# Attention inside a projection loop: own PSUM space for scores, rotary partners 64 rows apart, v stored twice

## The chip, the cores and the metric

One core of a Trainium2 chip runs the whole program. The metric is the time of one execution on the device in microseconds (us). TensorE (PE) multiplies, VectorE (DVE) and ScalarE (ACT) do the elementwise work, GpSimd (POOL) clears buffers, and SyncE (SP) issues the loads of weights. Each engine has its own stream of instructions, and they meet at semaphores.

## What is computed

Two layers over 256 tokens of width 2048, in fp32. Layer 0 mixes tokens by attention with 32 query heads and 4 key heads of width 64, rotary positions, a sink per head and a window of two chunks of 64; layer 1 by a recurrent block. Each is followed by a squared-ReLU MLP of width 8192. The change touches the attention alone:

```python
def rope(x, pos):
    half = x.shape[-1] // 2
    ...
    x1, x2 = xf[..., :half], xf[..., half:]
    out = jnp.concatenate([x1 * cos - x2 * sin, x2 * cos + x1 * sin], axis=-1)

    qkv = h @ w_qkv + b_qkv
    ...
    q = rope(q, pos)
    k = rope(k, pos)
    ...
    scores = jnp.where(valid, scores, NEG_INF)
    ...
    probs = jax.nn.softmax(jnp.concatenate([scores, sink], axis=-1), axis=-1)[..., :-1]
    out = jnp.einsum('bckgqs,bcskd->bcqkgd', probs.astype(v.dtype), v_band)
    out = out.reshape(B, S, N_HEADS * HEAD_DIM)
    return out @ w_o + b_o
```

## The kernel before

**Weights.** All projections stream 512 KB chunks of fp32 weights. ScalarE rounds a chunk to the fp32r type (`split_hi`, L343), VectorE takes the rest (`split_lo`, L766), and TensorE multiplies both parts. A *pair* is 256 output columns over all 16 row tiles: four `products` calls (s = 0 to 3) of 16 matmuls each, here called chunks of the pair. `next_hi` and `next_lo` prepare chunk s for the following pair as soon as the present pair has used its chunk s, since `w_hi` and `w_lo` hold one pair. At a pair's end ScalarE copies one half of the sum out of PSUM (`copy_half`, L356) and VectorE adds the other (`add_halves`, L780).

**The stage.** The projection to q, k and v is five quads of two pairs, q = 0 to 4. Quad 0 gives k and v. Of the others, each pair gives 256 columns of queries, which is four heads. Attention for the j-th such group runs one pair later, woven into the next pair's chunks. j = 0 lies in the pair (1, 1), j = 1 to 6 in the six pairs of quads 2 to 4, and j = 7 in the first quad of the output projection (`late_quad`, which has an order of its own). One *step* is one pair with the attention of one j.

**A step on TensorE.** Behind chunk 1: `rotate(j + 1)`, an fp32 product with a permutation matrix `swap` that puts each head's rotary partner, 32 rows away, in place, and `transpose_probs(j - 1)`, 8 transposes. Behind chunk 2: `scores(j)`, 24 matmuls of 256 columns, and `attend(j - 1)`, 24 matmuls of 128 columns. There, of two heads one takes rows 0 to 63 of the output and one rows 64 to 127. So `vcur` holds v between two blocks of zeros, and a slice of it that starts at v or in front of it sends v to the one half of the rows or the other. Scores and transposed probabilities share the two PSUM banks `xs`; the output of attend has a bank of its own, `x0`, and rotate one, `x3`.

**A step on VectorE**, in order: rotary multiply by cos (L858), multiply of the rotated copy in PSUM by sin (L863), their sum (L867); the low parts of the transposed probabilities (L898), of q (L872) and, in every other step, of v (L909); chunks 0 and 1 of the weights; `softmax_max(j)` (L881 to L885: a memset, a maximum and two small instructions, each waiting for the one ahead); chunk 2; `add_halves` and the scaling (L780, L853); `att_lo` (L903); `softmax_scale(j)` (L891 to L893), which waits for ScalarE's exponentials; chunk 3.

**A step on ScalarE:** the high parts of the same tiles, the eight exponentials of `softmax_exp` (L436, L438), `copy_half`, and the bias of q (L451, L452). The order on each engine is written out by hand in `attention_step`; nothing is reordered later.

## Time and profile before

| | us |
|---|---|
| Median of 3 runs | 2028.48 |
| Lowest and highest | 2027.62, 2029.05 |
| Profiled execution, its own time | 2027.66 |
| Its span, first to last instruction | 2025.7 |
| TensorE busy | 1999.9 |
| VectorE busy | 1358.7 |
| ScalarE busy | 1057.6 |

The span is that of one profiled execution. The stage of the change runs from 34.9 us, where the pair (1, 0) begins, to 215.9 us. The granted clock, PEclk, is a share of TensorE's full speed: 1.0 is 2.4 GHz, 0.5 is 1.2 GHz. In a timeline's row the number in brackets is how long the engine idled before the row, and who released it. A duration reaches into the next instruction's start where an engine overlaps them, so what an instruction costs is the distance between two starts.

### The profile page before, as it was taken

Reading aid. Unit: us, or ns where it says so; the run is one execution under the profiler, and the core shown is the slowest. Engines: PE = TensorE matmul, PEld = TensorE weight load, DVE = VectorE, ACT = ScalarE, POOL = GpSimd, SP = SyncE. Lnnn points to the kernel's source line nnn. Section 1 sums busy time; section 2 is a strip of 40 time slices with the busy share of each in tenths; the row PEclk is TensorE's granted clock in tenths of the full one; section 3 lists DMA queues with packets and bytes.
Section 4 is the critical chain, followed back from the end, with each engine's and each line's share of the span. In section 5 each row is a group of like instructions: output and inputs, shape, how many; then the busy total and the mean of one; then the engine's idle time right before and its main releaser. Section 6 shows DMA issues by size and latency. Waiting matters only on the chain.

```text
span 2025.7 us, 34215 instructions
## 1 busy us (share of the span) xinstructions
PE 1999.9 (99%) x11604; PEld 1747.6 (86%) x11604; DVE 1358.7 (67%) x1560; ACT 1057.6 (52%) x1438; POOL 8.7 (0%) x12
## 2 busy tenths in 40 slices
PE   9999999999999999999999999999999999999997
PEld 8888888888888888888888888888888888888886
DVE  7777676656655665667688887666566556656665
ACT  7555454444444444445588885544444444444453
POOL 1000000000000000000000000000000000000000
PEclk9999999999999999999999999999999999999998
DMA  8433556556565655565655555565566556555652
GB/s 276 141 104 115 195 169 207 190 184 193 180 197 177 199 190 188 180 195 175 209 178 185 180 166 183 176 207 187 186 186 187 195 178 197 187 188 178 202 171 90
DMA packets 365879, 368.12 MB, mean 182 GB/s; under 512 B 11536, under 2 KB 363920, under 8 KB 365712
## 3 DMA queue, kind: packets, MB, share of 16 engines
q1 hardware_dynamic: 365552, 365.53, 57.0%
q0 software_dynamic: 288, 2.10, 0.3%
q8 instruction: 22, 0.36, 0.1%
q14 instruction: 17, 0.14, 0.0%
HBM read 365.48 MB, written 2.10 MB: 181 GB/s over the span
## 4 chain that ended last, share of the span: by engine, by line
PE 90%; DVE 5%; ACT 2%; issue 2%; DMA 0%; DVEq 0%; ACTq 0%; SPq 0%
PE ps L1256 58%; PE ps L1259 29%; DVE w_lo L766 2%; PE aux L1276 1%; PE aux L1277 1%; PE aux L1278 1%; DVE xc L1145 0%; ACT L616 0%; DVE u L780 0%; PE aux L1292 0%; DVE v L1102 0%; PE aux L1329 0%; DMA h<-x_l_dram 0%; DVE h L1241 0%; ACT w_hi L343 0%
## 5 line engine op out<-in xcount | busy, mean ns | idle before, releaser
L766 DVE TENSOR_TENSOR w_lo<-w_raw,w_hi 128x1024 fp32r<-128x1024 f32 x678 | 816.7, 1223 | 336.3 <-ACT w_hi L343 335.2
L343 ACT ACTIVATE w_hi<-w_raw 128x1024 fp32r<-128x1024 f32 x678 | 701.7, 1054 | 434.7 <-PE ps L1259 432.1
L1256 PE MATMUL ps<-xn,w_hi 128*128 128x512 f32 x2880 | 908.4, 397 | 3.7 <-DVE xn L834 2.3
L1256 PE MATMUL ps<-mid,w_hi 128*128 128x512 f32 x2544 | 800.8, 396 | 1.9 <-DVE mid L903 1.5
L1259 PEld LDWEIGHTS ps<-xn,w_lo 128*128 128x128 f32 x2880 | 541.8, 188 | 128.3
L1259 PEld LDWEIGHTS ps<-mid,w_lo 128*128 128x128 f32 x2544 | 478.7, 188 | 113.2
L1259 PE MATMUL ps<-xn,w_lo 128*128 128x256 f32 x2880 | 566.7, 278 | 0.0
L1259 PE MATMUL ps<-mid,w_lo 128*128 128x256 f32 x2544 | 500.5, 278 | 0.0
L1256 PEld LDWEIGHTS ps<-xn,w_hi 128*128 128x128 f32 x2880 | 439.4, 189 | 5.8 <-issue 5.1
L1256 PEld LDWEIGHTS ps<-mid,w_hi 128*128 128x128 f32 x2544 | 388.0, 189 | 2.6 <-issue 2.6
L780 DVE TENSOR_TENSOR u<-ps,half 128x512 f32<-128x512 f32 x170 | 117.4, 691 | 182.9 <-ACT half L356 160.9
L356 ACT ACTIVATE half<-ps 128x512 f32<-128x512 f32 x154 | 91.8, 596 | 226.4 <-PE ps L1259 226.4
L565 ACT ACTIVATE mid<-u 128x512 f32 (+1 forms) x64 | 40.5, 633 | 105.5 <-DVE u L1018 105.5
L1024 DVE TENSOR_TENSOR mid<-v,mid 128x512 f32 (+1 forms) x64 | 44.3, 693 | 23.0 <-ACT mid L565 22.8
L806 DVE TENSOR_TENSOR h<-h,u 128x512 f32 (+1 forms) x70 | 48.5, 693 | 11.6 <-DVE u L780 11.5
L796 DVE SCALAR_TENSOR_TENSOR xn<-h,vec,xn (+1 forms) x48 | 21.2, 483 | 40.3 <-ACT xn L378 40.3
L1018 DVE SCALAR_TENSOR_TENSOR u<-u,rstd 128x512 f32<-128x512 f32 x64 | 44.3, 692 | 2.2
L1021 DVE TENSOR_TENSOR v<-u 128x512 f32<-128x512 f32 x64 | 44.2, 691 | 2.2
L376 ACT ACTIVATE sq<-h 128x512 f32 (+1 forms) x24 | 15.2, 633 | 41.5 <-DVE h L806 40.0
L1145 DVE SCALAR_TENSOR_TENSOR xc<-xb,vec,xc 128x256 f32<-128x256 f32 x48 | 21.1, 482 | 12.1 <-ACT xc L657 10.2
L785 DVE TENSOR_TENSOR acc<-acc,sq 128x512 f32<-128x512 f32 x31 | 21.3, 687 | 5.8 <-ACT sq L735 5.8
L359 ACT ACTIVATE half<-ps,vec 128x256 f32<-128x256 f32 x16 | 7.6, 473 | 28.8 <-PE ps L1259 28.8
(154 smaller groups left out, 808.2 us busy)
## 6 DMA issues: line engine op xcount, KB each, us to landing
w_raw<-mlp_w_up_dram SPq DMA_DIRECT2D x256, 512.0 KB, 3.8
w_raw<-mlp_w_down_dram SPq DMA_DIRECT2D x256, 512.0 KB, 3.4
w_raw<-b_w_in_dram SPq DMA_DIRECT2D x64, 512.0 KB, 4.9
w_raw<-a_w_qkv_dram SPq DMA_DIRECT2D x40, 512.0 KB, 5.2
w_raw<-a_w_o_dram SPq DMA_DIRECT2D x32, 512.0 KB, 3.7
w_raw<-b_w_out_dram SPq DMA_DIRECT2D x32, 512.0 KB, 4.4
h<-x_l_dram SPq DMA_DIRECT2D x4, 512.0 KB, 8.5
gate_raw<-b_gate_a_w_dram SPq DMA_DIRECT2D x8, 256.0 KB, 2.8
```

The source lines that it names most:

```text
L343: nc.scalar.activation(w_hi[:, s, :, :], w_raw[:, slot, :, :], ACT.Copy).then_inc(hi_ready, 1)
L356: nc.scalar.activation(half[:, :, :], src, ACT.Copy).then_inc(half_copied, 1)
L565: nc.scalar.activation(mid[:, 0, bass.ds(j * 2, 2), :], u[:, :, :], ACT.Square).then_inc(mid_hi, 1)
L766: nc.vector.tensor_tensor(w_lo[:, s, :, :], w_raw[:, slot, :, :], w_hi[:, s, :, :].bitcast(F32), ALU.subtract).then_inc(lo_ready, 1)
L780: nc.vector.tensor_tensor(u[:, :, :], ps[:, 2 * half_i:2 * half_i + 2, 0:TOK], half[:, :, :], ALU.add).then_inc(psum_free, 1)
L785: return nc.vector.tensor_tensor(acc[:, :, :], acc[:, :, :], sq[:, :, :], ALU.add)
L806: add = nc.vector.tensor_tensor(h_pair(j), h_pair(j), u[:, :, :], ALU.add)
L1018: nc.vector.scalar_tensor_tensor(u[:, :, :], in0=u[:, :, :], scalar=0.0, in1=bc2(rstd[:, :]), op0=ALU.max, op1=ALU.mult).then_inc(relu_rea ...
L1021: nc.vector.tensor_tensor(v[:, :, :], u[:, :, :], u[:, :, :], ALU.mult).then_inc(squared, 1)
L1024: nc.vector.tensor_tensor(mid[:, 1, bass.ds(j * 2, 2), :], v[:, :, :], mid[:, 0, bass.ds(j * 2, 2), :].bitcast(F32), ALU.subtract).then_in ...
L1256: nc.tensor.matmul(ps[:, 2 * half_i + b, :], hi[:, k, b * PART:(b + 1) * PART], operand[:, :, kt, :], start=kt == 0, stop=False)
L1259: last = nc.tensor.matmul(ps[:, 2 * half_i + b, TOK:2 * TOK], lo[:, k, b * PART:(b + 1) * PART], operand[:, 0, kt, :], start=False, stop=k ...
```

## The change

- **PSUM.** `xs`, the scores, takes banks 0 and 1. Transposed probabilities have banks 2 and 3, called `xt`, which the output of attend (`att_out`) then overwrites. Transposes of j - 1 now wait that the output of j - 2 has been read (`mid_ready`), and scores of j that the exponentials of j - 1 are done.
- **Rotary.** The host reorders the columns of `w_qkv` and its bias so that partners lie 64 rows apart in a tile. `rotate` is gone. VectorE multiplies by sin in two instructions of 64 rows, each reading one half of the rows and writing the other. Heads are now spread over the rows in blocks of 32, so keys are masked by a column of zeros and ones (`head_rows`), and one product with `swap` (`swap_keys`) serves the keys once; `kswap` is gone.
- **v twice.** `vcur` holds v two times side by side. `attend` is 12 matmuls of 256 columns: both heads of a pair share one stationary tile, and both halves of the output rows hold the same. `att_hi` and `att_lo` take rows 0 to 63 for one head and 64 to 127 for the other, in two instructions each. The split of v covers 512 elements a row where it covered 256.
- **Half a step later.** The softmax of j - 1 runs at the start of the pair that computes the scores of j. On TensorE `transpose_probs(j - 1)` stands behind chunk 2, and `scores(j)` and `attend(j - 1)` behind chunk 3. `rope(j + 2)` ends VectorE's step. In the last quad scores stand behind (0, 1), transposes behind (0, 2), attend of the last but one and the last transposes behind (1, 0), and the last attend behind (1, 1) where it stood behind (1, 2).

VectorE before, in the loop, from the rotary to the maximum (`h` holds the attention's small tiles, `aux` is PSUM):

```order
L858 TENSOR_TENSOR h<-u,const 128x512 [waits rope_in]
L863 TENSOR_TENSOR h<-aux,const 128x512 [waits rotated]
L867 TENSOR_TENSOR h<-h 128x512 [waits rot_read,cos_done]
L898 TENSOR_TENSOR pt<-aux,pt 128x1024 [waits pt_hi]
L872 TENSOR_TENSOR qz<-h,qz 128x4x2x64 [waits q_hi]
L765 ISA
L766 TENSOR_TENSOR w_lo<-w_raw,w_hi 128x1024 [waits hi_ready]
L765 REGISTER_ALU
L766 TENSOR_TENSOR w_lo<-w_raw,w_hi 128x1024 [waits hi_ready]
L881 MEMSET aux 64x2x2x64 [waits scored]
L760 REGISTER_ALU
L882 TENSOR_REDUCE h<-aux 128x8 [waits dve_step]
```

VectorE now, from the rotary's halves to the scaling of the probabilities:

```order
L875 TENSOR_TENSOR h<-u,const 64x512 x2
L877 TENSOR_TENSOR h<-h 128x512 [waits rope_terms]
L891 MEMSET aux 64x2x2x64 [waits scored]
L892 TENSOR_REDUCE h<-aux 128x8 [waits dve_step]
L893 SCALAR_TENSOR_TENSOR h<-h 128x8 [waits dve_step]
L895 TENSOR_TENSOR h<-vec,h 128x8 [waits dve_step]
L882 TENSOR_TENSOR qz<-h,qz 128x4x2x64 [waits q_hi]
L915 TENSOR_TENSOR mid<-aux,mid 64x4x2x64 [waits att_out_hi]
L915 TENSOR_TENSOR mid<-aux,mid 64x4x2x64
L901 TENSOR_TENSOR h<-h 128x8 [waits exp_done]
L902 RECIPROCAL h<-h 128x8 [waits dve_step]
L903 TENSOR_TENSOR h<-h 128x1024 [waits dve_step]
```

The rotary has lost its wait for TensorE and stands directly in front of the maximum, and the scaling follows the maximum with no chunk of weights between them.

ScalarE before, in the loop, from two chunks of weights to the copy of the pair's half:

```order
L342 REGISTER_ALU [waits raw_loaded6]
L343 ACTIVATE w_hi<-w_raw 128x1024 [waits wts_used]
L434 REGISTER_ALU
L436 ACTIVATE h<-h 128x8 [waits max_ready]
L438 ACTIVATE h<-aux,h 128x128 x4
L438 ACTIVATE h<-aux,h 128x128 [waits max_ready]
L438 ACTIVATE h<-aux,h 128x128 x3
L351 ISA
L356 ACTIVATE half<-ps 128x512 [waits psum_free,wts_used]
```

ScalarE now, from the end of one step to the first chunks of the next:

```order
L463 ACTIVATE mid<-aux 64x4x2x64 [waits att_done]
L463 ACTIVATE mid<-aux 64x4x2x64
L440 ACTIVATE qz<-h 128x4x2x64 [waits scored,roped]
L452 ACTIVATE h<-h 128x8 [waits max_ready]
L454 ACTIVATE h<-aux,h 128x128 x4
L454 ACTIVATE h<-aux,h 128x128 [waits max_ready]
L454 ACTIVATE h<-aux,h 128x128 x3
L357 ACTIVATE w_hi<-w_raw 128x1024 [waits wts_used,raw_loaded0]
L357 ACTIVATE w_hi<-w_raw 128x1024 [waits wts_used,raw_loaded1]
L357 ACTIVATE w_hi<-w_raw 128x1024 [waits wts_used,raw_loaded2]
L446 ACTIVATE pt<-aux 128x1024 [waits transposed]
```

The exponentials have moved from behind chunk 2 to the front of the step, ahead of all the weights.

The diff, cut to what the prediction speaks of:

```diff
-        x0, xs, x3 = aux[:, 0, :], aux[:, 1:3, :], aux[:, 3, :]
+        x0, xs, x3 = aux[:, 0, :], aux[:, 0:2, :], aux[:, 3, :]
+        xt = aux[:, 2:4, :]
+        att_out = xt.rearrange("p x (c b a t) -> p (x c) b a t", c=2, b=2, a=2)
...
+        swapped = x3.rearrange("p (b t) -> p b t", b=2)
+        key_places = ((0, 0, qa), (1, 1, qa), (0, 1, swapped), (1, 0, swapped))
+
+        def key_out(part, head, side):
+            return kpad[:, part, :, side, HD:HD + TOK].rearrange("p (b s) t -> p b s t", s=2)[:, :, head, :]
+
+        def att_place(part, j):
+            return mid[:, part, bass.ds(j * 2, 2), :].rearrange("p b (c t) -> p c b t", c=4)
+
+        def v_twice(part):
+            return vcur[:, part, :, :].rearrange("p c (s d) -> p c s d", s=2)
...
             def roped_hi(j):
                 act.wait_ge(roped, j + 2)
+                if not (isinstance(j, int) and j == 0):
+                    act.wait_ge(scored, j)
...
             def att_hi(j):
                 act.wait_ge(att_done, j + 1)
-                nc.scalar.activation(mid[:, 0, bass.ds(j * 2, 2), :], x0.rearrange("p (b t) -> p b t", b=2),
-                                     ACT.Copy).then_inc(att_out_hi, 1)
+                for a in range(2):
+                    r = slice(HD * a, HD * a + HD)
+                    last = nc.scalar.activation(att_place(0, j)[r], att_out[r, :, :, a, :], ACT.Copy)
+                last.then_inc(att_out_hi, 1)
...
+            for head, side, src in key_places:
+                last = nc.scalar.activation(key_out(0, head, side), src, ACT.Copy, scale=head_rows[:, side:side + 1])
...
             def attention_step(q, half_i, j):
-                next_hi(q, half_i, 0)
+                softmax_exp(j - 1, 0)
+                softmax_exp(j - 1, 1)
+                for s in range(3):
+                    next_hi(q, half_i, s)
                 pt_split_hi(j - 1)
-                roped_hi(j)
                 if half_i == 0:
                     act.wait_ge(v_read, 1)
                     vcur_split_hi(q - 2)
-                next_hi(q, half_i, 1)
-                next_hi(q, half_i, 2)
-                softmax_exp(j, 0)
-                softmax_exp(j, 1)
                 copy_half(q, half_i)
+                next_hi(q, half_i, 3)
+                q_bias(j + 1)
                 att_hi(j - 1)
-                q_bias(j + 1)
-                next_hi(q, half_i, 3)
-            with act.Fori(2, Q_QKV) as q:
+                roped_hi(j + 1)
+            attention_step(2, 0, 1)
+            attention_step(2, 1, 2)
+            with act.Fori(3, Q_QKV) as q:
...
-            def rope_cos(n):
+            def rope(n):
 
                 dve.wait_ge(rope_in, n + 1)
-                nc.vector.tensor_tensor(qa, u[:, :, :], bc2(cos), ALU.mult).then_inc(cos_done, 1)
-
-            def rope(n):
-
-                dve.wait_ge(rotated, n + 1)
-                nc.vector.tensor_tensor(qb, x3.rearrange("p (b t) -> p b t", b=2), bc2(sin), ALU.mult
-                                        ).then_inc(rot_read, 1)
-                dve.wait_ge(cos_done, n + 1)
-                dve.wait_ge(rot_read, n + 1)
+                nc.vector.tensor_tensor(qa, u[:, :, :], bc2(cos), ALU.mult).then_inc(rope_terms, 1)
+                for src, dst in ((slice(HD, PART), slice(0, HD)), (slice(0, HD), slice(HD, PART))):
+                    nc.vector.tensor_tensor(qb[dst], u[src, :, :], bc2(sin[src], HD), ALU.mult).then_inc(rope_terms, 1)
+                dve.wait_ge(rope_terms, n * 3 + 3)
...
             def att_lo(j):
                 dve.wait_ge(att_out_hi, j + 1)
-                nc.vector.tensor_tensor(mid[:, 1, bass.ds(j * 2, 2), :], x0.rearrange("p (b t) -> p b t", b=2),
-                                        mid[:, 0, bass.ds(j * 2, 2), :].bitcast(F32), ALU.subtract
-                                        ).then_inc(mid_ready, 1)
+                for a in range(2):
+                    r = slice(HD * a, HD * a + HD)
+                    last = nc.vector.tensor_tensor(att_place(1, j)[r], att_out[r, :, :, a, :],
+                                                   att_place(0, j)[r].bitcast(F32), ALU.subtract)
+                last.then_inc(mid_ready, 1)
...
+            def attention_step(q, half_i, j, att_before=True):
+                softmax_max(j - 1)
+                q_split_lo(j)
+                if att_before:
+                    att_lo(j - 2)
+                softmax_scale(j - 1)
+                next_lo(q, half_i, 0)
+                next_lo(q, half_i, 1)
                 pt_split_lo(j - 1)
-                q_split_lo(j)
+                next_lo(q, half_i, 2)
                 if half_i == 0:
                     vcur_split_lo(q - 2)
-                next_lo(q, half_i, 0)
-                next_lo(q, half_i, 1)
-                softmax_max(j)
-                next_lo(q, half_i, 2)
                 qkv_scale(q, half_i)
-                att_lo(j - 1)
-                softmax_scale(j)
                 next_lo(q, half_i, 3)
-            with repeat(dve, 2, Q_QKV, step, 10) as q:
+                rope(j + 2)
+            attention_step(2, 0, 1, False)
+            attention_step(2, 1, 2)
+            with repeat(dve, 3, Q_QKV, step, 10) as q:
...
-            def rotate(n):
-                pe.wait_ge(rope_in, n + 1)
-                nc.tensor.matmul(x3, swap, u[:, :, :], start=True, stop=True).then_inc(rotated, 1)
+            def swap_keys():
+                pe.wait_ge(roped, 1)
+                nc.tensor.matmul(x3, swap, qa, start=True, stop=True).then_inc(kswapped, 1)
...
-                    pe.wait_ge(pt_ready, j)
+                    pe.wait_ge(exp_done, j * 2)
...
+                if place is xt and not (isinstance(j, int) and j == 0):
+                    pe.wait_ge(mid_ready, j)
...
+                p_hi, p_lo = (pt[:, part, :, :].rearrange("p b (a c t) -> p c b a t", a=2, c=4) for part in range(2))
                 for c in range(4):
-                    out = x0.rearrange("p (b t) -> p b t", b=2)[:, :, c * HD:(c + 1) * HD]
-                    for a in range(2):
-                        v_cols = slice(HD, 3 * HD) if a == 0 else slice(0, 2 * HD)
-                        p_cols = slice(a * TOK + c * HD, a * TOK + (c + 1) * HD)
-                        last = three(out, vcur[:, 0, c, v_cols], vcur[:, 1, c, v_cols],
-                                     pt[:, 0, :, p_cols], pt[:, 1, :, p_cols], a == 0, a == 1)
+                    last = three(att_out[:, c], vcur[:, 0, c, :], vcur[:, 1, c, :], p_hi[:, c], p_lo[:, c], True, True)
...
-                pair(q, half_i, *qkv, {1: lambda: rotate_and_transpose(j, g_before is not None),
-                                       2: lambda: scores_and_output(j, g, g_before)})
+                between = {3: lambda: scores_and_output(j, g, g_before)}
+                if g_before is not None:
+                    between[2] = lambda: transpose_probs(j - 1)
+                pair(q, half_i, *qkv, between)
...
-            late_quad(QB_WO, att, {(0, 0): lambda: rotate(last_j + 1),
-                                   (0, 1): lambda: transpose_probs(last_j - 1),
-                                   (0, 2): lambda: scores_and_output(last_j, last_g, last_g),
-                                   (1, 1): lambda: transpose_probs(last_j),
-                                   (1, 2): lambda: attend(last_j, last_g)})
+            def attend_and_transpose():
+                attend(last_j - 1, last_g)
+                transpose_probs(last_j, xs, late_prob)
+
+            late_quad(QB_WO, att, {(0, 1): lambda: scores(last_j, last_g),
+                                   (0, 2): lambda: transpose_probs(last_j - 1),
+                                   (1, 0): attend_and_transpose,
+                                   (1, 1): lambda: attend(last_j, last_g)})
```

## Rows read from the trace of the kernel before

**Rows 1.** First row of the page: busy time and share of each engine.

```profile
PE 1999.9 (99%) x11604; PEld 1747.6 (86%) x11604; DVE 1358.7 (67%) x1560; ACT 1057.6 (52%) x1438; POOL 8.7 (0%) x12
```

**Rows 2.** TensorE's waits, 0 to 240 us: sum, times, longest, us.

```profile
PE aux L1276 <- DVE qz L872: 2.8, 7, 1.2
...
PE ps L1256 <- DVE mid L903: 1.5, 1, 1.5
...
PE aux L1292 <- ACT u L452: 0.9, 2, 0.5
```

**Rows 3.** Timeline of TensorE: start, duration, line, out<-in, count.

```profile
60.45 0.63 PE L1256 MATMUL ps<-xn,w_hi 128*128 128x512 f32 x2
...
81.09 0.68 PE L1256 MATMUL ps<-xn,w_hi 128*128 128x512 f32 x2
...
88.81 0.62 PE L1256 MATMUL ps<-xn,w_hi 128*128 128x512 f32 x2
...
89.51 1.02 PE L1292 MATMUL aux<-u,const 128*128 128x512 f32 x2
90.37 1.04 PE L1329 MATMUL aux<-const,h 128*128 128x128 f32 x8
91.16 0.72 PE L1256 MATMUL ps<-xn,w_hi 128*128 128x512 f32 x2
...
94.47 0.38 PE L1276 MATMUL aux<-kpad,qz 128*128 x1 [0.26 <-DVE qz L872]
...
97.43 0.22 PE L1276 MATMUL aux<-pt,vcur 128*128 128x128 f32 x1
...
100.07 0.68 PE L1256 MATMUL ps<-xn,w_hi 128*128 128x512 f32 x2
```

**Rows 4.** Timeline of VectorE, the parts of one step.

```profile
103.74 0.69 DVE L780 TENSOR_TENSOR u<-ps,half 128x512 f32<-128x512 f32 x1 [2.68 <-ACT half L356]
104.47 0.69 DVE L853 TENSOR_TENSOR u<-u,rstd 128x512 f32<-128x512 f32 x1
105.08 0.69 DVE L903 TENSOR_TENSOR mid<-aux,mid 128x512 f32 x1
105.68 0.16 DVE L891 TENSOR_TENSOR h<-h 128x8 f32<-128x8 f32 x1
...
106.10 1.22 DVE L893 TENSOR_TENSOR h<-h 128x1024 f32<-128x1024 f32 x1
107.25 1.22 DVE L766 TENSOR_TENSOR w_lo<-w_raw,w_hi 128x1024 fp32r<-128x1024 f32 x1
...
109.54 0.69 DVE L863 TENSOR_TENSOR h<-aux,const 128x512 f32<-128x512 f32 x1 [0.48 <-PE aux L1292]
110.34 0.69 DVE L867 TENSOR_TENSOR h<-h 128x512 f32<-128x512 f32 x1
...
113.22 0.42 DVE L909 TENSOR_TENSOR vcur<-vraw,vcur 128x256 fp32r<-128x256 f32 x1
...
116.71 0.27 DVE L881 MEMSET aux<- 64x256 f32 x1 [0.80 <-PE aux L1278]
```

**Rows 5.** Timeline of ScalarE: from the first exponential's row to the copy behind.

```profile
118.91 0.21 ACT L436 ACTIVATE h<-h 128x8 f32<-128x8 f32 x1 [4.63 <-DVE h L885]
...
122.09 0.60 ACT L356 ACTIVATE half<-ps 128x512 f32<-128x512 f32 x1 [0.18 <-PE ps L1259]
```

**Rows 6.** Timeline of VectorE: instructions of 64 rows, at both halves.

```profile
45.05 2.59 DVE L937 TENSOR_TENSOR kpad<-h,kpad 64x512 fp32r<-64x512 f32 x4 [2.04 <-ACT kpad L487]
```

**Rows 7.** Timeline of TensorE: behind its two longest waits in this stage.

```profile
75.48 0.38 PE L1276 MATMUL aux<-kpad,qz 128*128 x1 [1.24 <-DVE qz L872]
...
208.77 0.86 PE L1256 MATMUL ps<-mid,w_hi 128*128 128x512 f32 x2 [1.50 <-DVE mid L903]
```

**Rows 8.** Busy time and granted clock (PEclk) in stretches behind those waits.

```profile
73.00:77.00 4.00, 2.76 (x20) 2.43 (x19) 4.00 (x6) 2.83 (x4) 0.00 (x0) 1.00 0.38 125
...
209.00:212.40 3.40, 3.40 (x12) 2.88 (x12) 1.10 (x1) 0.00 (x0) 0.46 (x1) 0.52 0.67 193
```

More of the change, by code:

```diff
@@ L1450, in _rope_tables, with _halves_apart @@
     cos = np.cos(ang).astype(np.float32).T[p % half]
[L1451 removed]
+    sin = np.sin(ang).astype(np.float32).T[p % half] * np.where(p < HD, 1.0, -1.0)[:, None]
     swap = np.zeros((PART, PART), np.float32)
     swap[p, p ^ half] = 1.0
[L1454 removed]
+    head = (p // half) % 2
+    rows = np.stack([head == 0, head == 1], axis=1)
+    return np.concatenate([cos, sin, swap, np.eye(PART), rows], axis=1).astype(np.float32)
+def _halves_apart(a):
+    heads = a[..., :(HEADS + KV_HEADS) * HD]
+    pairs = heads.reshape(*heads.shape[:-1], -1, 2, 2, HD // 2).swapaxes(-3, -2)
+    return np.concatenate([pairs.reshape(heads.shape), a[..., heads.shape[-1]:]], axis=-1)
 def _columns(a):
```

145 lines of the change are left out of this document (64 added, 81 removed).

## Prediction

> **What bounds the kernel now.** I read the busy shares first. TensorE is busy for 1999.9 of 2025.7 us [rows 1], so outside the attention only TensorE's work and waits count, and the change doesn't touch them there. In the stage of the change TensorE's waits come next [rows 2]: seven for the split queries (2.8 us together), one for the last output of attention (1.5 us) and two for the biased queries (0.9 us). Then the timeline of one step [rows 3]. From one pair's last chunk to the next pair's it is 100.07 - 81.09 = 18.98 us. Four matmuls of the projection take 89.51 - 88.81 = 0.70 us, sixteen such groups 11.1 us. Rotate takes 90.37 - 89.51 = 0.86 us, the transposes 91.16 - 90.37 = 0.79 us, scores 97.43 - 94.47 = 2.96 us, attend 100.07 - 97.43 = 2.64 us. The reader is to see that some 7 us of each step are attention on the engine that sets the time. Last, VectorE and ScalarE in that step [rows 4, 5]: not full, but soon close to it.
>
> **What leaves TensorE.** Rotate ran nine times and the key swap runs once, with the same operand sizes: 8 x 0.86 = 6.9 us. Attend ran 24 matmuls of 128 columns in 2.64 us, 0.110 us each, and now runs 12 of 256. The nearest row for those is scores, 24 matmuls of 256 columns in 2.96 us, of which a filled pipeline makes 0.120 us each: 12 x 0.120 = 1.44 us, a saving of 1.20 us, eight times 9.6 us. Transposes and scores stay as they are.
>
> The page "TensorE: Matmul & The Clock Gate" of the Trainium skill (section "Back-to-back issue gap") gives for an isolated matmul a spacing that goes with the columns, some 56 ns for 128 and 109 ns for 256. By that attend would be 1.3 us before and after, and the merge worth nothing. The trace differs: 110 ns for 128 columns.
>
> **A step's work on TensorE** is then 18.98 - 0.86 - 1.20 - 0.42 = 16.50 us, where 0.42 us is the wait for q in front of scores, 0.26 us idle [rows 3] and the refill: four groups from 91.16 us and the transposes' drain of 0.1 us would have let scores start at 94.05 us. That wait goes: `rope(j + 2)` now ends two steps ahead of its use.
>
> **What VectorE gets.** The rotary's multiply by sin becomes two instructions of 64 rows. Each has as many elements a row as the one of 128 rows, so each costs as much: four such instructions took 2.59 us [rows 6], 0.65 us each, on the upper and the lower half alike. None of them read one half and wrote the other; no row of VectorE shows that. From below such an instruction costs 0.6 us, as any of 512 elements [rows 4]; from above I take twice the row, 1.3 us. I take 0.65 us. `att_lo` is doubled as well, +0.6 us, and the split of v, 0.42 us [rows 4], goes to that of 512 elements, 0.6 us, every other step.
>
> **The new ring.** Between the step's parts there is now a closed chain through VectorE and ScalarE, and I add it up from [rows 4, 5]. From the memset to the first exponential 118.91 - 116.71 = 2.20 us. The exponentials 3.00 us (to 121.91 us, 0.18 us ahead of the copy). Scaling, 107.25 - 105.68 = 1.57 us. Chunks 0 and 1 of the weights, the low parts of the probabilities, chunk 2: all of 1024 elements a row like the row at 106.10 us, 107.25 - 106.10 = 1.15 us each, 4.6 us. Adding halves and scaling 0.73 + 0.61 us, chunk 3 1.15 us. The rotary: 0.6 for cos, 0.65 and 0.80 for the halves (the second is waited for, as the row from 109.54 to 110.34 shows), 0.6 for the sum. That is 16.5 us, and 17.1 us in a step with v. Then the memset of the next softmax follows at once. The split of q and both halves of `att_lo` (1.8 us) lie beside the 3.0 us of exponentials, where VectorE waits anyway, so **the doubled att_lo costs nothing**; if that cover went, it would cost 0.6 us a step. On ScalarE the doubled `att_hi` stands before the exponentials, and ends before the rotary does, which they need.
>
> So the ring and TensorE are nearly level: 16.5 us in one step, 17.1 us in the next, 16.8 us on average, where TensorE alone would do 16.5 us. The wait moves to the transposes, which need the scaled probabilities: about 0.1 us and 0.7 us in turn.
>
> **The sum by stretches.**
> - Pair (1, 0) to the end of (1, 1): two rotates go (-1.7 us), the key swap comes (+0.9), the wait for the first q goes (-0.4), and VectorE's longer rotary makes two short waits (+0.4): -0.8 us.
> - The first of six steps. It was 81.09 - 60.45 = 20.6 us long [rows 3], with waits of 1.24 us [rows 7] and 0.5 us. Now the softmax of j = 0 begins only when VectorE has finished the rotary behind the pair (1, 1). Memset about 3.8 us into the pair, 5.2 us to the end of the exponentials and 1.6 us of scaling make 10.8 us, and TensorE is behind chunk 2 after 8.4 us. It waits for 2.4 us; the step is 18.9 us. -1.7 us.
> - Five more steps: 5 x (18.98 - 16.8) = -10.9 us.
> - The last quad. Rotate and its wait go (-1.4), attend twice (-2.4), the wait for the last output of attention with its refill (-1.7): that attend stands one chunk, 2.8 us, earlier. Two waits come. `scores(7)` stands behind the second chunk, 5.6 us into the quad, and needs the exponentials of j = 6, which end at about 6.8 us: +1.2 us. `attend(6)` then stands 9.4 us behind the start of scores(7). But the split of its probabilities is queued on ScalarE behind the exponentials of j = 7: 3.8 us to VectorE's memset, 2.2, 3.0, 1.0 for the high parts, 1.2 for the low, 0.6 for v, 11.8 us in all: +2.4 us. Small ones +0.4. Together -1.5 us.
> - The clock. Behind the wait of 1.50 us, from 208.77 us [rows 7], TensorE ran until 212.4 us at a granted clock of 0.52 [rows 8], which is its 1.2 GHz; 3.6 us at half speed hold 1.9 us of work and cost 1.7 us. With that wait gone: -1.7 us.
>
> Sum -16.6 us. Against this the two new waits of 2.4 us, both longer than 1.50 us. I charge each with a low stretch. In the first step half of the loss hides in the following wait for the ring, so 1.3 us; in the last quad, less hidden, 1.5 us. Net -13.8 us. The profiled execution took 2027.7 us, which gives 2013.9 us. The median of the three runs lies 0.8 us above that execution; halfway between, I say **2014.3 us**.
>
> Of the clock the page "TensorE: Matmul & The Clock Gate" (section "Why this matters for your kernels") asks only for gaps longer than either of these to be avoided; by it neither stretch would come. The trace speaks against it at 208.77 us and for it at 75.48 us, where 1.24 us of waiting left the clock at 1.00.
>
> **Rivals.**
> - *No low stretch, or a shorter ring.* For it: the clock of 1.00 behind 1.24 us [rows 8]. Against: 0.52 behind 1.50 us. Time: 2027.7 - 16.6 = 2011.1 us; were the ring covered fully, 5 x 0.3 us less, 2010 us. Chance 0.22.
> - *VectorE becomes the bound for good.* If an instruction that reads one half of the rows and writes the other costs 1.3 us, the ring is 1.3 us longer, 18.1 us. Seven steps lose 9 us: about 2023 us; half of that, 2019 us. For it: nothing shows such an instruction. Against: the equal durations on both halves [rows 6]. Chance 0.14.
> - *Attend doesn't shrink.* Its moving operand is now gathered from four runs of 64 columns where it had two. If 256 columns in such runs took 0.22 us, attend would stay at 2.64 us, TensorE's step at 17.7 us, and the time at 2014 + 7 x 0.9, about 2020 us. Chance 0.05.
> - *Slower than before: the clock stays low in the steps.* The transposes' wait recurs in each step. If waits of 0.7 us, with transposes and short matmuls around them, kept TensorE at 1.2 GHz, a step's 16.5 us would be up to 33 us. One low stretch of 1.7 us in each of eight steps gives 13.6 us back (2025 us without the two charged); from 10 such stretches on nothing is left of 16.6 us, from 13 on the kernel is slower by over 0.2%, and with the clock low throughout the steps it would be above 2080 us. For it: the stretch behind 1.50 us. Against: seven waits for q of 0.26 to 1.24 us left no low clock. Chance 0.04.
>
> **How the numbers follow.** The forecast has the remaining 0.55 and spans 2012.5 to 2017.5 us: its own uncertainty is 0.2 us a step. The range takes in the first rival and the better half of the second and third: 2009.5 to 2021 us. What a measurement can tell is 0.2%, 4 us. Faster by more than that: all but the slower rival and a part of those at 2023 us, 0.93. Same: 0.03. Slower: 0.04.
>
> **What would show it.** In the changed kernel's trace the attend matmuls of 256 columns at 0.120 us; a step of 16.5 and 17.1 us in turn; TensorE's largest waits at the transposes, for VectorE's scaling, and two of about 2.4 us, at the first transposes and at attend in the last quad; the granted clock around 0.5 behind them; no wait at the last quad's fourth chunks. VectorE's idle time should sit in front of `softmax_scale` alone, about 1.4 us. It is wrong if the rotary's halves last longer than 0.8 us, if attend's matmuls stand 0.2 us apart, or if the low clock comes back in the steps.

## The result, and the profile after

The changed kernel takes 2015.65 us (median of 4 executions, 2014.61 to 2015.79), the kernel before beside it 2028.19 us (4 executions, 2027.62 to 2029.05). The ratio is 0.9943, 95% interval [0.9931, 0.9954]: 12.5 us gained, where 14.2 us were forecast. The profiled execution took 2015.68 us, its span 2013.8 us.

The first row of the page after, busy time and share of each engine:

```profile
PE 1983.1 (98%) x11492; PEld 1736.1 (86%) x11492; DVE 1371.6 (68%) x1577; ACT 1062.4 (53%) x1444; POOL 7.4 (0%) x11
```

TensorE has 16.8 us less to do than in [rows 1], VectorE 12.9 us more. TensorE's waits in the changed kernel, 0 to 240 us, as in [rows 2] (sum, times, longest, us):

```profile
PE aux L1339 <- DVE h L903: 6.3, 6, 2.5
...
PE aux L1284 <- DVE pt L908: 2.1, 1, 2.1
PE aux L1284 <- ACT h L454: 1.4, 1, 1.4
```

The waits for the split queries, for the biased queries and for the last output of attention are gone. The waits now stand at the transposes (L1339), for VectorE's scaled probabilities (L903), six times. The two single ones are the last quad's scores and attend. Where they stand, in TensorE's timeline (start, duration, line, out<-in, count; in brackets how long it idled ahead and for whom):

```profile
73.82 1.09 PE L1339 MATMUL aux<-const,h 128*128 128x128 f32 x8 [2.52 <-DVE h L903]
...
91.07 1.09 PE L1339 MATMUL aux<-const,h 128*128 128x128 f32 x8 [0.69 <-DVE h L903]
...
125.72 1.09 PE L1339 MATMUL aux<-const,h 128*128 128x128 f32 x8 [1.00 <-DVE h L903]
...
160.43 1.09 PE L1339 MATMUL aux<-const,h 128*128 128x128 f32 x8 [0.98 <-DVE h L903]
...
175.63 0.36 PE L1284 MATMUL aux<-kpad,qz 128*128 128x256 f32 x1 [1.42 <-ACT h L454]
...
187.34 0.36 PE L1284 MATMUL aux<-pt,vcur 128*128 128x256 f32 x1 [2.13 <-DVE pt L908]
```

With the two rows left out (108.16 us, 0.53 us of waiting, and 142.87 us, 0.58 us) the distances are the steps: 17.25, 17.09, 17.56, 17.15 and 17.56 us. The last four are 17.1 us and, with the split of v, 17.6 us in turn. The first has v in it too, but its two steps stand outside the loop, where VectorE's small instructions behind the maximum lie closer (1.46 us from the maximum to the second of them, 84.54 to 86.00 us, where the loop takes 1.72 us, 136.00 to 137.72 us). The changed kernel's 256-column attend matmuls:

```profile
97.79 0.28 PE L1285 MATMUL aux<-pt,vcur 128*128 128x256 f32 x1
97.91 0.28 PE L1286 MATMUL aux<-pt,vcur 128*128 128x256 f32 x1
```

They start 0.12 us apart. One step of VectorE after, with v in it, to be read against [rows 4]:

```profile
132.80 0.69 DVE L873 TENSOR_TENSOR h<-u,const 128x512 f32<-128x512 f32 x1
133.52 1.41 DVE L875 TENSOR_TENSOR h<-u,const 64x512 f32<-64x512 f32 x2
134.96 0.69 DVE L877 TENSOR_TENSOR h<-h 128x512 f32<-128x512 f32 x1
135.70 0.27 DVE L891 MEMSET aux<- 64x256 f32 x1
...
138.44 1.38 DVE L915 TENSOR_TENSOR mid<-aux,mid 64x512 f32 x2
141.07 0.17 DVE L901 TENSOR_TENSOR h<-h 128x8 f32<-128x8 f32 x1 [1.25 <-ACT h L454]
...
147.33 0.68 DVE L921 TENSOR_TENSOR vcur<-vraw,vcur 128x512 fp32r<-128x512 f32 x1
...
150.45 0.69 DVE L873 TENSOR_TENSOR h<-u,const 128x512 f32<-128x512 f32 x1
```

VectorE idles in one place that matters, 1.25 us in front of the scaling. The rest of the ring is work, and it is closed after 150.45 - 132.80 = 17.65 us.

The clock in the changed kernel, behind the first wait and behind the longest one of the last quad (columns as in [rows 8]; the ninth value is the granted clock):

```profile
73.80:77.20 3.40, 3.38 (x22) 3.07 (x23) 3.40 (x4) 2.65 (x4) 0.00 (x0) 1.00 0.29 73
187.30:190.70 3.40, 3.36 (x19) 3.39 (x20) 2.57 (x4) 1.55 (x3) 0.00 (x0) 0.62 0.00 0
190.70:194.00 3.30, 3.30 (x19) 2.89 (x18) 2.99 (x4) 2.09 (x3) 0.00 (x0) 0.87 0.53 159
```

Behind 2.52 us of waiting TensorE went on at 2.4 GHz; behind 2.13 us it ran a good part of 6.7 us at 1.2 GHz.

Where the time went, by the starts of the pairs in both traces (the last row ends at TensorE's first matmul on `gate_hi`, 213.19 us before and 201.35 us after):

| stretch | before | after | change | forecast, with its clock charges |
|---|---|---|---|---|
| start to pair (2, 0) | 63.24 | 62.77 | -0.5 | -0.8 |
| first step | 20.70 | 19.09 | -1.6 | -1.7 + 1.3 |
| five steps | 94.91 | 86.62 | -8.3 | -10.9 |
| last quad | 34.34 | 32.87 | -1.5 | -1.5 - 1.7 + 1.5 |
| sum | | | -11.8 | -13.8 |

Nearly the whole gain, 11.8 us of 12.0 us between the two profiled executions, is in the stage.

### The profile page after: what moved, and what is told of

Its sections match the earlier page's. It is cut to its first block, busy times and chain, and to the rows that moved or that the text cites. A ratio compares the mean times of both kernels' runs of the same rounds, so it can differ in the third digit from the quotient of the medians.

```text
span 2013.8 us, 33942 instructions
## 1 busy us (share of the span) xinstructions
PE 1983.1 (98%) x11492; PEld 1736.1 (86%) x11492; DVE 1371.6 (68%) x1577; ACT 1062.4 (53%) x1444; POOL 7.4 (0%) x11
## 4 chain that ended last, share of the span: by engine, by line
PE 85%; DVE 9%; ACT 3%; issue 3%; DMA 0%; DVEq 0%; ACTq 0%; SPq 0%
PE ps L1264 56%; PE ps L1267 28%; DVE w_lo L781 3%; ACT h L454 1%; DVE h L875 1%; DVE u L795 1%; DVE h L892 0%; DVE xc L1153 0%; ACT L631 0%; DVE v L1110 0%; DVE h L903 0%; PE aux L1284 0%; DMA h<-x_l_dram 0%; PE aux L1286 0%; PE aux L1285 0%
## 5 line engine op out<-in xcount | busy, mean ns | idle before, releaser
L454 ACT ACTIVATE h<-aux,h 128x128 f32<-128x128 f32 x64 | 22.4, 375 | 0.1
```

The source lines that it names most:

```text
L454: last = nc.scalar.activation(out[:, m * PART:(m + 1) * PART], xs[:, b, (m % 4) * PART:(m % 4 + 1) * PART], ACT.Exp, bias=s_neg[:, m:m + 1 ...
```

## The experiments

My theory: TensorE's saving is real, but the time is set by a ring through VectorE and ScalarE, so the order on VectorE is worth as much as the matmuls, and the distance from my forecast is the ring's mis-sized parts. The rival: VectorE's changes are hidden, and the missing gain is TensorE's own, its clock above all. The kernel before ran beside every variant, and each ratio is to it: its median was 2027.94 us (17 executions) beside the rotary alone, the rotary with v twice, attend in 24 matmuls and the rotary in the cover, and 2026.31 us (13 executions) beside the other four.

**The rotary part alone.** The kernel before, with only the exchange of rows and the rotary without TensorE; order, v and PSUM as before.

```diff
-                nc.vector.tensor_tensor(qb, x3.rearrange("p (b t) -> p b t", b=2), bc2(sin), ALU.mult
-                                        ).then_inc(rot_read, 1)
+                for src, dst in ((slice(HD, PART), slice(0, HD)), (slice(0, HD), slice(HD, PART))):
+                    nc.vector.tensor_tensor(qb[dst], u[src, :, :], bc2(sin[src], HD), ALU.mult).then_inc(rope_terms, 1)
...
-            late_quad(QB_WO, att, {(0, 0): lambda: rotate(last_j + 1),
-                                   (0, 1): lambda: transpose_probs(last_j - 1),
+            late_quad(QB_WO, att, {(0, 1): lambda: transpose_probs(last_j - 1),
```

> The kernel before with the rotary part of the change alone: columns reordered, VectorE multiplies by sin in two halves, TensorE swaps the keys once, and the order of every step stays that of before (cos now stands where it stood, directly ahead of the halves). Theory A, that the chain through VectorE and ScalarE sets a step once TensorE has less to do: the query's chain in a step grows by one halves instruction (0.7 us) while TensorE reaches scores 0.86 us earlier, so the wait for q in front of scores grows from 0.3 to about 1.2 us a step and a step stays near 18.9 us; the total is 2028 to 2031 us, no gain at all. Rival B, that TensorE's work alone sets the time and what leaves it is gained in full: 8 x 0.86 = 6.9 us less, 2021 us.

Measured 2030.38 us (10 executions, 2027.77 to 2031.58), ratio 1.0012 [1.0002, 1.0021]. TensorE's timeline of this variant, three of its waits:

```profile
75.91 0.38 PE L1268 MATMUL aux<-kpad,qz 128*128 x1 [2.27 <-DVE qz L869]
...
94.56 0.38 PE L1268 MATMUL aux<-kpad,qz 128*128 x1 [0.78 <-DVE qz L869]
...
188.92 0.36 PE L1268 MATMUL aux<-kpad,qz 128*128 128x256 f32 x1 [1.92 <-DVE pt L895]
```

TensorE's rotate is gone (0.86 us a step), and the step shrinks only from 18.98 to 18.64 us (94.56 to 113.20 us, the next such row). The rest comes back as a wait for the queries: 0.78 us where it was 0.26 [rows 3], 2.27 us in the first step where it was 1.24 [rows 7]. In the old order q stands behind VectorE's rotary. The end of that chain before, and the chain in this variant:

```profile
111.48 1.23 DVE L898 TENSOR_TENSOR pt<-aux,pt 128x1024 fp32r<-128x1024 f32 x1 [0.45 <-ACT pt L430]
112.62 0.68 DVE L872 TENSOR_TENSOR qz<-h,qz 128x512 fp32r<-128x512 f32 x1
```

```profile
107.33 1.22 DVE L768 TENSOR_TENSOR w_lo<-w_raw,w_hi 128x1024 fp32r<-128x1024 f32 x1
...
112.37 0.68 DVE L869 TENSOR_TENSOR qz<-h,qz 128x512 fp32r<-128x512 f32 x1
```

From the chunk of weights ahead of the rotary to q's low part it took 112.62 - 107.25 = 5.37 us [rows 4], with 0.93 us of waiting in it (0.48 us for rotate [rows 4] and 0.45 us for ScalarE), and takes 112.37 - 107.33 = 5.04 us with none: the second half has filled most of that waiting. So q comes 0.33 us earlier, where TensorE could take it 0.86 us earlier. I had expected the chain to grow, with a wait of 1.2 us. The last quad adds a wait of 1.92 us with a granted clock of 0.67 behind it (189 to 193 us), and in this trace the stage ends 0.7 us earlier than before, TensorE's first matmul on `gate_hi` standing at 212.47 us. So one part that takes 6.9 us of work off the engine that is 99% busy brings nothing, against the rival. The clock isn't the reason: at a mean granted clock of 0.996 or above this variant takes 2027.8 and 2028.3 us and the kernel before 2025.2 to 2026.4 us, at 0.994 or 0.995 they take 2029.0 to 2031.6 and 2027.7 to 2028.9 us.

**The rotary and v twice, in the old order.** All of the changed kernel but the half step, with the PSUM banks laid out so that it fits.

```diff
-        x0, xs, x3 = aux[:, 0, :], aux[:, 1:3, :], aux[:, 3, :]
+        x0, xs, x3 = aux[:, 0, :], aux[:, 2:4, :], aux[:, 1, :]
+        att_out = aux[:, 0:2, :].rearrange("p x (c b a t) -> p (x c) b a t", c=2, b=2, a=2)
...
-                    for a in range(2):
...
-                        last = three(out, vcur[:, 0, c, v_cols], vcur[:, 1, c, v_cols],
-                                     pt[:, 0, :, p_cols], pt[:, 1, :, p_cols], a == 0, a == 1)
+                    last = three(att_out[:, c], vcur[:, 0, c, :], vcur[:, 1, c, :], p_hi[:, c], p_lo[:, c], True, True)
```

> The kernel before with the rotary part and with v twice (attend in 12 matmuls of 256 columns, its output in two PSUM banks of its own), but with the order of every step as before: the change without its half step. TensorE has 16.4 us less to do in all than before. Theory A: the wait for q grows to about 2.1 us a step, a wait of 0.5 us for the scaled probabilities comes, a step stays near 19.1 us, 2029 to 2034 us: slower than before or equal, so that the new order of the softmax carries the whole gain. Rival B: the two savings on TensorE count in full, 2012 us. Rival C, that each part gives its share and the order gives the rest: about 2020 us.

Measured 2040.37 us (2038.96 to 2042.2), ratio 1.0065 [1.0048, 1.0082]: slower than before, by more than either expectation. TensorE's timeline from one step of this variant to the next, and the stretch behind the longer wait (start:end, us, busy times, the ninth value the granted clock):

```profile
117.83 0.38 PE L1278 MATMUL aux<-kpad,qz 128*128 x1 [1.97 <-DVE qz L878]
...
138.63 0.38 PE L1278 MATMUL aux<-kpad,qz 128*128 x1 [1.95 <-DVE qz L878]
```

```profile
118.00:122.00 4.00, 4.00 (x22) 4.00 (x23) 2.55 (x3) 0.90 (x1) 0.00 (x0) 0.57 0.27 90
```

VectorE's timeline there, at the maximum that waits for the scores:

```profile
143.38 0.27 DVE L887 MEMSET aux<- 64x256 f32 x1 [2.62 <-PE aux L1280]
```

The step is 138.63 - 117.83 = 20.80 us. Two waits of 2.5 us together stand in it (0.53 us again at the transposes in between), and behind the longer one the scores run at 1.2 GHz, in five of the six steps (the granted clock is 0.57 to 0.69 over the 4 us behind it). Half speed also delays the maximum, 2.62 us here, and with it what the next waits are for. This is the mechanism of my slower rival, a low clock that recurs in the steps; the changed kernel escapes it, this order doesn't. An estimate: 4 us at a clock of 0.57 cost 1.7 us. If none of that hides in a wait, the step would be the 19.1 us of the theory without it, and the time, less five such stretches, some 2032 us. So up to 8 us of the 25 us to the changed kernel are the low clock, and the rest is the order. Against before, the other two parts cost 12 us without the half step and the PSUM space that comes with it, and with them all three gain 12.5 us. The half step by itself was not run, and neither was the new PSUM space in the old order, so how the gain divides between those two isn't shown.

**Attend with 24 matmuls of 128 columns.** The changed kernel; v stays twice, the moving operand is halved.

```diff
-                    last = three(att_out[:, c], vcur[:, 0, c, :], vcur[:, 1, c, :], p_hi[:, c], p_lo[:, c], True, True)
+                    for a in range(2):
+                        last = three(att_out[:, c, :, a, :], vcur[:, 0, c, :], vcur[:, 1, c, :],
+                                     p_hi[:, c, :, a, :], p_lo[:, c, :, a, :], True, True)
```

> The changed kernel with attend again in 24 matmuls of 128 columns (the same products, each head's columns by themselves). TensorE's step grows from 16.5 to about 17.7 us, against a ring through VectorE and ScalarE of 17.1 and 17.6 us in turn as measured in the changed kernel. Theory A: each of the five steps between the first and the last quad grows only from 17.35 to 17.7 us, so the steps lose about 2 to 3 us, and with the last quad's two attends about 4 us are lost: 2018 to 2020 us, and the wait at the transposes falls below 0.2 us. Rival B, TensorE's work counts in full: 8 x 1.2 = 9.6 us, 2025 us. If attend's spacing went with its columns (128 columns at 0.06 us), nothing would change: 2015.6 us.

Measured 2022.77 us (8 executions, 2018.37 to 2023.44), ratio 0.9973 [0.9962, 0.9984], between the two expectations. Its timeline and its clock behind the first wait:

```profile
73.68 1.09 PE L1339 MATMUL aux<-const,h 128*128 128x128 f32 x8 [2.54 <-DVE h L903]
...
92.86 1.04 PE L1339 MATMUL aux<-const,h 128*128 128x128 f32 x8
...
110.46 1.04 PE L1339 MATMUL aux<-const,h 128*128 128x128 f32 x8
```

```profile
74.00:78.00 4.00, 4.00 (x19) 3.42 (x17) 4.00 (x4) 2.30 (x3) 0.00 (x0) 0.60 0.48 136
```

The step is 17.60 us (92.86 to 110.46 us) with no wait in it: TensorE's own work, 16.5 + 1.2 = 17.7 us by my sum, now covers the ring. In the changed kernel it was 17.3 us. So of the 1.20 us that attend gives back in a step, only some 0.3 us reach the time while the ring is 17.3 us long; the rest goes into the wait. The other part of the difference is clock. Two of the eight executions took 2018.4 and 2018.5 us at a mean granted clock of 0.996, the other six 2021.6 to 2023.4 us at 0.993 or 0.994. The profiled one is of the latter, with a low stretch behind the first wait that the changed kernel's trace lacks behind the same wait. My expectation of 2018 to 2020 us holds for the first group alone.

**One multiply by sin of 128 rows.** The changed kernel, with the exchange of rows left out, so that the rotary isn't computed.

```diff
-                for src, dst in ((slice(HD, PART), slice(0, HD)), (slice(0, HD), slice(HD, PART))):
-                    nc.vector.tensor_tensor(qb[dst], u[src, :, :], bc2(sin[src], HD), ALU.mult).then_inc(rope_terms, 1)
-                dve.wait_ge(rope_terms, n * 3 + 3)
+                nc.vector.tensor_tensor(qb, u[:, :, :], bc2(sin), ALU.mult).then_inc(rope_terms, 1)
+                dve.wait_ge(rope_terms, n * 2 + 2)
```

> The changed kernel with the multiply by sin done by one instruction of 128 rows, each row with its own element: the exchange of the two halves is left out, so the rotated values are not the reference's. It takes one instruction of 0.72 us off VectorE and nothing off TensorE. Theory A, the ring sets the step: 0.72 us a step and another 0.12 us for each start that follows an instruction on other rows; the steps fall from 17.1 and 17.6 us towards TensorE's own 16.5 us, 0.75 us each for five, 1 us in the first and 0.5 us in the last quad: 2010 to 2011 us. Rival B, TensorE's order sets it: 2015.6 us. In the trace, cos to sin and sin to the sum: 0.6 us from start to start in place of 0.72 us, if the extra 0.1 us comes from changing the rows.

Measured 2008.51 us (2008.28 to 2008.53), ratio 0.9911 [0.9894, 0.9927]. VectorE's rotary, and TensorE's timeline in this variant:

```profile
127.79 0.69 DVE L873 TENSOR_TENSOR h<-u,const 128x512 f32<-128x512 f32 x1
128.40 0.68 DVE L874 TENSOR_TENSOR h<-u,const 128x512 f32<-128x512 f32 x1
129.12 0.69 DVE L876 TENSOR_TENSOR h<-h 128x512 f32<-128x512 f32 x1
129.85 0.27 DVE L890 MEMSET aux<- 64x256 f32 x1
```

```profile
71.11 1.09 PE L1338 MATMUL aux<-const,h 128*128 128x128 f32 x8 [0.91 <-DVE h L902]
...
168.26 0.35 PE L1283 MATMUL aux<-kpad,qz 128*128 128x256 f32 x1 [0.60 <-ACT h L454]
```

From cos to the memset it is 2.06 us where it was 2.90. An instruction on VectorE, 0.84 us a step, is worth 6 to 7 us in all (by the ratios and by the medians), though VectorE is busy 68% of the span. That is the plainest evidence for the ring: the rival expected 2015.6 us. I expected 2010 to 2011 us and undershot the gain: the first wait falls by 1.6 us (2.52 to 0.91 us) and that of the last quad's scores by 0.8 us (1.42 to 0.60 us), where I had counted 1 us and 0.5 us.

**Two instructions of 64 rows that cross nothing.** The changed kernel, each half multiplied in its own rows, so that again the rotary isn't computed.

```diff
-                for src, dst in ((slice(HD, PART), slice(0, HD)), (slice(0, HD), slice(HD, PART))):
+                for src, dst in ((slice(0, HD), slice(0, HD)), (slice(HD, PART), slice(HD, PART))):
```

> The changed kernel with the two instructions of 64 rows writing the rows that they read: the exchange of halves is left out, so the rotated values are not the reference's. The number of instructions and rows is unchanged. The changed kernel's trace has 0.72 us from the start of cos to the first half and 0.72 us to the second, where 0.61 us stand between instructions of 128 rows. Theory A1, the extra 0.11 us is paid when an instruction starts on other rows than the one ahead: here cos and the first half both start at row 0, so that distance falls to 0.61 us and the second stays 0.72 us; the ring is 0.1 us shorter, 2015 us. Rival A2, reading one half and writing the other costs it: both fall to 0.61 us, 2014.5 us. In either case the total moves by at most 1 us, so the rotary's halves as such cost a whole instruction each.

Measured 2013.74 us (2013.25 to 2014.63), ratio 0.9938 [0.9921, 0.9954]. VectorE's rotary in this variant:

```profile
130.89 0.69 DVE L873 TENSOR_TENSOR h<-u,const 128x512 f32<-128x512 f32 x1
131.50 1.40 DVE L875 TENSOR_TENSOR h<-u,const 64x512 f32<-64x512 f32 x2
132.93 0.69 DVE L877 TENSOR_TENSOR h<-h 128x512 f32<-128x512 f32 x1
```

The two halves take 1.43 us where the crossing ones take 1.44. Crossing itself costs nothing; what it changes is the start of the first half, 0.61 us behind cos where it stood 0.72 us behind. That is 0.11 us a step, and the steps agree, 17.0 and 17.4 us for 17.1 and 17.6. I had expected at most 1 us in all. Between the medians it is 1.9 us, by the two ratios to the kernel before 1.0 us; each step's 0.13 us over nine rotaries makes 1.2 us, and what is left can't be told from the spread of the executions.

**The low part of the output outside the exponentials' cover.** The changed kernel with `att_lo` behind the scaling.

```diff
+                softmax_scale(j - 1)
                 if att_before:
                     att_lo(j - 2)
-                softmax_scale(j - 1)
```

> The changed kernel with one thing moved: the two instructions of att_lo stand behind softmax_scale, outside the 1.3 us in which VectorE waits for the exponentials. Theory A: in the cover they cost nothing and outside it they cost the ring their 1.3 us in each of five steps: 2015.6 + 6.5 = 2022 us; the wait at the transposes grows to 1.8 and 2.3 us in turn, now for mid, and such waits may bring TensorE's 1.2 GHz back, up to 2030 us. Rival B, VectorE has slack and the place doesn't matter: 2015.6 us.

Measured 2022.64 us (10 executions, 2021.57 to 2023.38), ratio 0.9979 [0.9969, 0.9989], as the theory had it. VectorE's timeline, and TensorE's, in this variant:

```profile
128.51 0.17 DVE L901 TENSOR_TENSOR h<-h 128x8 f32<-128x8 f32 x1 [2.58 <-ACT h L454]
...
130.09 1.38 DVE L915 TENSOR_TENSOR mid<-aux,mid 64x512 f32 x2
131.51 2.36 DVE L781 TENSOR_TENSOR w_lo<-w_raw,w_hi 128x1024 fp32r<-128x1024 f32 x2
```

```profile
131.62 1.06 PE L1339 MATMUL aux<-const,h 128*128 128x128 f32 x8 [2.56 <-DVE mid L915]
...
169.12 1.06 PE L1339 MATMUL aux<-const,h 128*128 128x128 f32 x8 [2.56 <-DVE mid L915]
```

VectorE's idle time in front of the scaling grows from 1.25 to 2.58 us, `att_lo` lies on the ring with 1.42 us, and two steps take 169.12 - 131.62 = 37.5 us, 18.75 us each where it was 17.3. So in the changed kernel all of `att_lo` is hidden, its doubling too.

**The rotary in the cover as well.** If the 1.25 us of idle time are real cover, something on the ring can move in. The changed kernel, with the rotary behind the maximum, and the low parts of q and of the output behind the scaling (ScalarE's high part of q follows the exponentials).

```diff
                 softmax_max(j - 1)
-                q_split_lo(j)
+                rope(j + 1)
+                softmax_scale(j - 1)
                 if att_before:
                     att_lo(j - 2)
-                softmax_scale(j - 1)
+                q_split_lo(j)
...
-                rope(j + 2)
```

> The changed kernel with one thing moved: the rotary of q stands behind the softmax's maximum instead of ahead of it, in the 3 us in which VectorE waits for the exponentials; the high and low parts of q and the output's low part follow the scaling. No work is added or removed. Theory A: the 2.9 us of the rotary leave the ring, VectorE's own work is 16.1 us a step, TensorE's 16.5 us sets it, and the wait at the transposes goes nearly to zero, in the first step too: five steps less 0.85 us each and the first less 2.5 us, 7 us in all, 2009 us; the first part of the last quad waits longer for q (2.5 us where 1.4 us). Rival B, that the waits at the transposes come from TensorE's own order: no change, 2015.6 us. Rival C, that the maximum then waits for scores: half of it, 2012 us.

Measured 2009.53 us (2008.31 to 2010.0), ratio 0.9911 [0.9894, 0.9927], as expected. TensorE's timeline of this variant, steps and the last quad:

```profile
86.35 1.06 PE L1339 MATMUL aux<-const,h 128*128 128x128 f32 x8
...
102.73 1.04 PE L1339 MATMUL aux<-const,h 128*128 128x128 f32 x8
...
119.42 0.85 PE L1339 MATMUL aux<-const,h 128*128 128x128 f32 x6 [0.17 <-DVE mid L915]
...
152.48 1.06 PE L1339 MATMUL aux<-const,h 128*128 128x128 f32 x8 [0.16 <-DVE mid L915]
...
169.10 0.39 PE L1284 MATMUL aux<-kpad,qz 128*128 128x256 f32 x1 [2.85 <-DVE qz L882]
```

Two steps take 33.06 us (119.42 to 152.48 us), 16.53 us each. A step that starts and ends without a wait takes 16.38 us (86.35 to 102.73 us): that is TensorE's own work, which I had put at 16.50 us. The others, with a wait of 0.17 us for the output's low part, take 16.69 us. So the steps are within 0.3 us of their floor, and the next limit stands in the last quad, where q is now late: 2.85 us.

**The last quad mended.** The same, with q's low part in the last quad directly behind its rotary, and ScalarE's high part of the probabilities of j = 6 ahead of the exponentials of j = 7.

The edit against the variant ahead:

```diff
-            softmax_exp(last, 0, late_prob)
-            softmax_exp(last, 1, late_prob)
...
+            softmax_exp(last, 0, late_prob)
+            softmax_exp(last, 1, late_prob)
...
+            q_split_lo(last)
             softmax_scale(last - 1)
             att_lo(last - 2)
-            q_split_lo(last)
```

> The kernel with the rotary in the exponentials' cover (2009.5 us), changed in the last quad alone: VectorE takes the low part of the last q directly behind its rotary, and ScalarE splits the probabilities of j = 6 ahead of the exponentials of j = 7. In that kernel's trace TensorE waits in the last quad 2.9 us for q and 1.5 us for the split probabilities. Theory A, those two waits are chains of order alone: the first falls to 0.2 us, the second to 0.5 us, and a new one of 2 us comes at the last transposes, since their exponentials are later: 2 us less, 2007.5 us. Rival B, the last quad's chain only moves its wait: 2009.5 us.

Measured 2006.75 us (2006.66 to 2007.41), ratio 0.9902 [0.9885, 0.9918], the fastest of all, 8 to 9 us below the changed kernel. TensorE's longest wait left in this stage, at the last transposes (sum, times, longest, us):

```profile
PE aux L1339 <- DVE h L903: 1.5, 1, 1.5
```

The wait for q has gone from 2.85 to 0.4 us, that for the probabilities in front of attend (1.49 us) has gone, and one of 1.5 us has come at the last transposes. The low clock that followed the 2.85 us (0.66 from 168 to 173 us) is gone from the trace too; how much of the 2 to 3 us gained over the variant ahead is the clock isn't shown.

## Why the prediction was right, and where it wasn't

The time lies 1.35 us above the forecast. Point by point:

**TensorE's work: right.** Attend's matmuls stand 0.12 us apart as taken from the row of scores, and the busy time fell by 16.8 us [rows 1] against 16.5 us for rotate and attend (each of the two traces has one low stretch in its busy time). A step without waits was to be 16.50 us; the rotary in the cover shows 16.38 us, so the sum was 0.1 us long.

**The ring: the mechanism was right, the size too small.** It was to be 16.5 and 17.1 us and is 17.1 and 17.6. ScalarE's timeline after, from the exponentials' start to the work behind them:

```profile
137.92 0.21 ACT L452 ACTIVATE h<-h 128x8 f32<-128x8 f32 x1 [1.60 <-DVE h L895]
...
140.89 2.99 ACT L357 ACTIVATE w_hi<-w_raw 128x1024 fp32r<-128x1024 f32 x3
```

The rotary was put at 2.65 us and takes 135.70 - 132.80 = 2.90 us: both halves, the sum and the memset behind it each start only when what is ahead is over, 0.72 to 0.74 us apart, where I had 0.65 or 0.6 us for all but one (0.80). Exponentials to scaling were 3.00 us in the sum and are 3.15 us (141.07 less 137.92, the first row above): I had left out that VectorE starts 0.18 us after ScalarE is free for its next work. The other parts together were 0.14 us short, in pieces of 0.02 to 0.07 us. The new v is 0.60 us as taken. That is 0.5 us a step. TensorE waited 0.5 to 0.7 us and 1.0 us in turn, not 0.1 and 0.7, and the five steps brought 8.3 us instead of 10.9.

**att_lo doubled at no cost: right**, by the experiment that takes it out of its cover. The idle time there was to be 1.4 us and is 1.25.

**The first step: right in size, in part by luck, and wrong in its clock.** It was to be 18.9 us and a charge of 1.3 us; it is 19.09 us with a wait of 2.52 us for the forecast 2.4, and no low clock behind it in this trace. The three terms of that wait, 3.8, 5.2 and 1.6 us, add up to 10.6 us and not to the 10.8 us that the sum goes on with. Measured it is 10.91 us (62.77 to 73.68 us): the memset came 4.33 us into the pair, 0.5 us later than taken, and the exponentials ended 4.82 us behind it, 0.4 us sooner.

**The last quad: right.** Waits of 1.42 and 2.13 us where 1.2 and 2.4 were forecast, a low stretch behind the longer one, and -1.5 us in all against -1.7.

**The clock: half right, and not to be foretold by the length of a wait.** One of the two charged stretches came. In the sum this miss (-1.3 us) hid half of the ring's (+2.6 us); without that luck the time would have been 2017 us, still within the range of the forecast case. The low stretch before, which the sum took as certain to be there and to go (-1.7 us), is itself a matter of chance, as the last section shows. All four executions of the kernel before that stand beside the changed kernel (2027.62 to 2029.05 us) are of the slower of its two groups of executions; against the faster, 2025.2 to 2026.4 us, the change gains some 10 us and not 12.5.

**The rivals.** *Slower by a low clock in the steps* was no idle thought: the other two parts in the old order do just that, at 2040 us. *VectorE the bound for good* was half right in that VectorE's ring sets the steps; but a crossing instruction costs 0.72 us, not 1.3. *Attend doesn't shrink* is ruled out by the 0.12 us between its matmuls.

## What to carry to other kernels

Before taking work from the busiest engine, close the loop through the others: add up, start to start, the chain from one step's result back to itself. Here 6.9 us of matmuls removed were worth nothing in the old order, while 0.84 us a step on an engine that is 68% busy were worth 6 to 7 us. Then look for the one place where that chain idles, and move into it what lies on the chain and isn't needed at once: that gained 6 us, and 2 to 3 us more once the order of the last quad had followed, with the same instructions.

## What the runs showed of the hardware

**A start on other rows.** A VectorE instruction of 512 elements starts 0.61 us behind its like when both start at row 0 (cos, then sin in the variants that don't cross). It starts 0.72 us behind when it reads from row 64 on where the one ahead read from row 0, with no semaphore between them. Its own length doesn't change, and neither does it matter that it writes to other rows than it reads. The Trainium skill, page "VectorE: DVE Perf Modes", section "Two Vector instructions with no wait between them", says that an instruction is held until all earlier ones are finished if its inputs or its output start in another quadrant than the last ones did. The traces agree, with 0.11 us for it here.

**The clock.** The same wait of some 2.5 us at the first transposes was followed by a granted clock of 1.00 in the changed kernel and of 0.60 with attend in 24 matmuls. In the variant with `att_lo` outside the cover a wait of 2.08 us in the second step was followed by 0.61, while the next four, of 1.75 to 2.56 us, left it at 1.00 from 100 to 200 us. Waits of 1.95 us in front of the scores brought it down to 0.57 to 0.65 in four steps of the old order with both parts, and left it at 1.00 in the fifth. And the kernel before itself comes in two groups: of its 30 executions beside the variants, 13 took 2025.2 to 2026.4 us at a mean granted clock of 0.996 or 0.997, and 17 took 2027.7 to 2028.9 us at 0.994 or 0.995. The two are about as far apart as the one low stretch behind 208.77 us [rows 8] costs, and the rotary alone, with the same wait of 1.5 us in that place, showed a clock of 1.00 there (and 0.67 behind its wait of 1.92 us). That the slower group is the one with this stretch is likely but not shown: only one execution of the kernel before has a trace. So a stretch of low clock behind a wait of 1.5 to 2.5 us is a chance of some 2 us, not a certainty. What decides it, beyond the length of the wait, stayed open; no experiment was made on it alone.

The Trainium skill, page "TensorE: Matmul & The Clock Gate", section "Why this matters for your kernels", asks only for gaps longer than any of these to be avoided; these traces show 1.2 GHz behind 1.50 us [rows 7, 8] and behind 2.13 us.

Not tried either: v twice without the rotary part, since rotate's bank, two of scores and two of attend don't fit beside each other.
